# One-hot rows of four tokens: one compare on VectorE and one multiply on GpSimd

## The chip, the core and the metric

The kernel runs on one core of a Trainium2 chip. The metric is the time on the device in microseconds, from the first to the last instruction of one execution and what little lies around them. Three runs of the kernel before took 3524.62, 3525.51 and 3529.61 us; the median is 3525.51.

## What is computed

The reference is a model of two blocks for 512 tokens of width 1024, all in float32. The first block mixes (pooling and a gated delta rule) and then runs a product-key expert layer; the second block is a state-space and attention hybrid. The change lies in the expert layer alone. There every token has 8 heads x 16 = 128 picks; each pick has a first key, a second key (both 0 to 127) and a gate:

```python
experts = jnp.take_along_axis(cand_idx, pos, axis=-1)   # = first * 128 + second
gates = jax.nn.softmax(top_score, axis=-1)
u = jnp.take(expert_down, ei, axis=0)
act = jax.nn.gelu(jnp.einsum("btd,bthkd->bthk", xi, u), approximate=False)
vv = jnp.take(expert_up, ei, axis=0)
return jnp.einsum("bthk,bthkd->btd", gi * act, vv)
```

The kernel does not gather. It computes all 128 x 128 experts for every token and weights them by a gate matrix of 128 x 128 numbers for each token, which is zero but at the token's picks. That matrix is a product of two one-hot matrices. With the 128 picks of a token on the partitions, row p of the one is 1 at pick p's second key, row p of the other is the gate at pick p's first key, and TensorE's product of the two, summed over the picks, is the gate matrix.

## The kernel before

The program is a list of stages. `run` calls each and puts a barrier of all engines behind it, so no instruction of a stage starts before the last one of the stage ahead of it is done. Three stages matter.

`peer_pick` finds the picks of each 128 tokens and transposes them by TensorE, so that picks lie on partitions and tokens along the free dimension: `first`, `second` and `gate`, each 128 x 512. It fills them by three copies out of PSUM (L1443). GpSimd writes `count`, the numbers 0 to 127 in every partition (L1356). In the same stage VectorE compares and multiplies tiles of 128x2048 (L1420, L1427) and reduces them (L1433), while GpSimd subtracts tiles of the weight stream in `split_low` (L162), 128x1024 each.

`peer_gates` is the stage that the change is in. It goes through the 512 tokens four at a time (`QUAD`), 128 steps in all; the buffers `hot1`, `hot2` and four PSUM banks hold four steps. In each step:

- VectorE waits until the product of four steps back is made, then writes the four rows of `hot1`, each by one instruction with two operations, compare `count` with the token's first keys and multiply by its gates (L1498). Keys and gates are scalars of the partition, read from `first` and `gate`. Then it writes the third row of `hot2` by a compare with `second` (L1502).
- GpSimd writes the first two rows of `hot2` by compares (L1487), with scalars from `now`, a copy of the next 16 columns of `second` that it makes itself every fourth step (L1479).
- ScalarE writes the fourth row of `hot2` in two instructions, the absolute distance of the key from the count (L1526) and then 1 minus that, cut at zero (L1532).
- TensorE waits for all three makers and for a free bank, and multiplies, 128x128x128 in float32 for each token (L1517). The profile has two records for each product, so 1024 in all.
- ScalarE copies the bank of four tokens into `stage`, transposed within the partition (L1550). After 32 tokens SyncE stores the 2 MB of `stage` to memory (L1560), from where the next stages load them.

Order within an engine is that of the program: `steps` is a hardware loop whose body has four steps. Everything else is held by semaphores: `product` counts TensorE's steps, `second_made`, `first_made` and `third_made` the makers', `read` the evictions. `past` waits and then counts up a second semaphore of its own engine.

`peer_early` and `peer_experts` follow. They use the stored gate matrices, not `first`, `second` or `gate`.

Of the kernel before, what the change touches and what calls it, by code (L numbers as in the profile page):

```python
# [15 lines left out]
ALU = mybir.AluOpType  # L16
ACT = mybir.ActivationFunctionType
# [5 lines left out]
P = 128  # L23
D = 1024
S = 512
# [1283 lines left out]
QUAD = 4  # L1309
AHEAD = 4 * QUAD  # L1310


def peer_pick(g):
# [7 lines left out]
    g.first = g.at("first", R + 17, [P, S])  # L1321
    g.gate = g.at("gate", R + 18, [P, S])

    g.second = g.at("second", R + 19, [P, S + AHEAD])
# [21 lines left out]
    with ExitStack() as stack:  # L1346
# [5 lines left out]
        with nc.Block() as block:  # L1352
            @block.gpsimd
            def _(pool):
                pool.memset(g.second[:, S:], 0.0)
# [40 lines left out]
            def _(dve):  # L1396
                dve.wait_ge(counted, 1)
                dve.sem_inc(kept, 1)
                with steps(dve, 0, TT, 1) as t:
# [42 lines left out]
                    for r, out in enumerate((g.first, g.second, g.gate)):  # L1442
                        dve.tensor_copy(out[:, bass.ds(t * P, P)], bank[:, r * P:r * P + P]).then_inc(kept, 1)  # L1443
# [6 lines left out]
def peer_gates(g):  # L1450
# [5 lines left out]
    BY_POOL = 2  # L1456
    n_groups = S // GROUP
    g.gates = nc.dram_tensor("gates", [n_groups, P, N_KEYS, GROUP], F32, kind="Internal").ap()
    hot2 = g.at("hot2", R + 21, [P, 4, QUAD, N_KEYS])
    hot1 = g.at("hot1", R + 25, [P, 4, QUAD, N_KEYS])  # L1460
    now = g.at("now", R + 16.5, [P, 4 * QUAD])
    now_read, passed = g.sem("now_read"), g.sem("passed")
    stage = [g.at(f"stage{s}", R + 8 * s, [P, N_KEYS, GROUP]) for s in range(2)]
    second_made, first_made, third_made, product, read, apart, act_passed = (g.sem(x) for x in (
        "second_hot", "first_hot", "second_hot_by_act", "product", "read", "apart", "act_passed"))
    stored = [g.sem(f"stored{s}") for s in range(2)]
    quads = GROUP // QUAD
    with ExitStack() as stack:
        banks = g.banks(stack, 4, "gates")

        with nc.Block() as block:
            @block.gpsimd
            def _(pool):
                pool.sem_inc(product, 4)
                pool.sem_inc(second_made, 1)
                with steps(pool, 0, S // QUAD, 4) as i:

                    pool.wait_ge(second_made, i + 1)
                    pool.tensor_copy(now[:, :], g.second[:, bass.ds(i * QUAD, 4 * QUAD)]).then_inc(now_read, 1)  # L1479
                    pool.wait_ge(now_read, i // 4 + 1)  # L1480
                    for j in range(4):

                        pool.wait_ge(product, i + (j + 1))
                        pool.sem_inc(passed, 1)
                        for k in range(BY_POOL):
                            n = j * QUAD + k
                            ins = pool.tensor_scalar(hot2[:, j, k, :], g.count[:, :], now[:, n:n + 1], None,  # L1487
                                                     ALU.is_equal)
                        ins.then_inc(second_made, 1)

            @block.vector
            def _(dve):
                with steps(dve, 0, S // QUAD, 4) as i:
                    for j in range(4):
                        dve.wait_ge(product, i + (j + 1))
                        for k in range(QUAD):
                            t = i * QUAD + (j * QUAD + k)
                            ins = dve.tensor_scalar(hot1[:, j, k, :], g.count[:, :], g.first[:, bass.ds(t, 1)],  # L1498
                                                    g.gate[:, bass.ds(t, 1)], ALU.is_equal, ALU.mult)
                        for k in range(BY_POOL, QUAD - 1):  # L1500
                            t = i * QUAD + (j * QUAD + k)
                            ins = dve.tensor_scalar(hot2[:, j, k, :], g.count[:, :], g.second[:, bass.ds(t, 1)],  # L1502
                                                    None, ALU.is_equal)

                        ins.then_inc(first_made, 1)
# [16 lines left out]
            def _(act):  # L1522
# [14 lines left out]
                for j in range(4):  # L1537
                    distance(0, j)
                    last_row(0, j)
# [1024 lines left out]
```

## Time and profile before

| | |
|---|---|
| median of three runs | 3525.51 us |
| the profiled execution: its span, first to last instruction | 3527.5 us |
| PE, PEld busy | 3129.7, 2511.6 us |
| DVE, ACT, POOL busy | 1958.1, 1223.1, 446.7 us |
| the gates stage | 1136.8 to 1322.6 us of the span |

The profiled execution has no other time of its own than its span; the span lies between the shortest and the longest of the three runs. PE is TensorE's matmuls, PEld its weight loads, DVE is VectorE, ACT ScalarE, POOL GpSimd and SP SyncE. A busy time is the time in which at least one instruction of the engine was listed as running, waits within the instruction included. In a group of lines the sum after the bar is the busy time, the next number the mean of one instruction in ns, and behind the second bar is the idle time of the engine just before them, with what ended it. A row of the timeline may hold several instructions (x4); its duration is then from the start of the first to the end of the last.

### The profile page before, as it was taken

The page shows a single profiled execution, that of the slowest core. Times are in us where ns is not written, and L with a number is a line of the kernel's source. Part 1 is how long each engine was busy: PE and PEld are TensorE (multiplying, and loading weights), DVE is VectorE, ACT ScalarE, POOL GpSimd, SP SyncE. Part 2 cuts the span into 40 slices and gives each one's busy share as a digit, 9 for nine tenths or more (in the row PEclk, how much of TensorE's full clock was granted, in tenths as well). Part 3 has the DMA queues.
Part 4 walks back from the last instruction along what each step waited for, and adds up shares of the span by engine and source line. Part 5 has one row for each costly group of instructions (what it writes and reads, how often), then busy time and mean ns, then how long its engine had stood idle before and what let it go on. Part 6 is the DMA issues. An engine that isn't in the chain of part 4 may idle for free. (4 is left out here: it accounts for less than half of the span.)

```text
span 3527.5 us, 46718 instructions
## 1 busy us (share of the span) xinstructions
PE 3129.7 (89%) x14568; PEld 2511.6 (71%) x14568; DVE 1958.1 (56%) x3602; ACT 1223.1 (35%) x1758; POOL 446.7 (13%) x656
## 2 busy tenths in 40 slices
PE   6987886996888777999999999999979787888996
PEld 5866784875676666788888888888857566655785
DVE  2555554335999986755555555555554673222232
ACT  3342122432233772222223222222233332466342
POOL 1002333000045990000000000000000130012000
PEclk9999997998998998999999999999989898988998
DMA  2210001321121444433333333333322102200321
GB/s 106 95 65 1 0 0 51 107 94 55 65 84 60 182 175 155 128 122 119 119 119 119 119 119 124 121 122 122 123 84 95 48 25 72 71 0 0 107 95 66
DMA packets 136387, 311.73 MB, mean 88 GB/s; under 512 B 9104, under 2 KB 74768, under 8 KB 134160
## 3 DMA queue, kind: packets, MB, share of 16 engines
q1 hardware_dynamic: 136160, 311.00, 26.0%
q8 instruction: 24, 0.39, 0.0%
q10 hardware_dynamic: 176, 0.11, 0.0%
q14 instruction: 27, 0.22, 0.0%
HBM read 273.33 MB, written 37.75 MB: 88 GB/s over the span
## 5 line engine op out<-in xcount | busy, mean ns | idle before, releaser
L153 ACT ACTIVATE split<-raw 128x1024 fp32r<-128x1024 f32 x440 | 455.7, 1055 | 1250.4 <-PE up L1138 457.6
L162 DVE TENSOR_TENSOR split<-raw,split 128x1024 fp32r<-128x1024 f32 x408 | 491.7, 1224 | 604.6 <-ACT split L153 595.1
L1136 PE MATMUL up<-split,weight_high 128*128 128x512 f32 x1024 | 400.4, 391 | 21.1 <-DVE weight_low L1668 21.1
L1137 PE MATMUL up<-split,weight_high 128*128 128x512 f32 x1024 | 399.1, 390 | 0.0
L1138 PE MATMUL up<-split,weight_low 128*128 128x512 f32 x1024 | 398.9, 390 | 0.0
L1814 DVE TENSOR_TENSOR h<-h,up 128x512 f32<-128x512 f32 x416 | 269.4, 684 | 108.0 <-PE up L1138 108.0
L1750 PE MATMUL down<-xh,split 128*128 128x512 f32 x832 | 323.8, 389 | 1.9 <-ACTq L1771 1.9
L1752 PE MATMUL down<-xh,split 128*128 128x512 f32 x832 | 323.7, 389 | 0.0
L1751 PE MATMUL down<-xl,split 128*128 128x512 f32 x832 | 323.6, 389 | 0.0
L177 PE MATMUL proj<-xh,split 128*128 128x512 f32 x640 | 250.6, 392 | 28.5 <-ACTq L440 28.5
L178 PE MATMUL proj<-xl,split 128*128 128x512 f32 x640 | 250.2, 391 | 0.0
L179 PE MATMUL proj<-xh,split 128*128 128x512 f32 x640 | 250.2, 391 | 0.0
L1136 PEld LDWEIGHTS up<-split,weight_high 128*128 128x128 f32 x1024 | 192.6, 188 | 65.1 <-issue 21.3
L1138 PEld LDWEIGHTS up<-split,weight_low 128*128 128x128 f32 x1024 | 192.5, 188 | 40.2
L1137 PEld LDWEIGHTS up<-split,weight_high 128*128 128x128 f32 x1024 | 192.6, 188 | 39.7
L2048 POOL TENSOR_TENSOR dec<-dec,upto 128x512 f32<-128x512 f32 x16 | 20.1, 1277 | 1490.5 <-ACT dec L2039 1490.5
L1799 DVE TENSOR_TENSOR weight<-gelu,gate 128x512 f32<-128x512 f32 x104 | 72.0, 692 | 246.2 <-ACT gelu L1780 246.2
L1517 PE MATMUL gates<-hot,hot 128*128 128x128 f32 x1024 | 145.6, 290 | 41.0 <-DVE hot L1502 20.6
L1750 PEld LDWEIGHTS down<-xh,split 128*128 128x128 f32 x832 | 156.2, 188 | 34.7 <-ACTq L1771 2.3
L1752 PEld LDWEIGHTS down<-xh,split 128*128 128x128 f32 x832 | 156.2, 188 | 32.4
L1751 PEld LDWEIGHTS down<-xl,split 128*128 128x128 f32 x832 | 156.2, 188 | 32.4
L1517 PEld LDWEIGHTS gates<-hot,hot 128*128 128x128 f32 x1024 | 126.1, 194 | 60.6 <-DVE hot L1502 39.5
(397 smaller groups left out, 5678.0 us busy)
## 6 DMA issues: line engine op xcount, KB each, us to landing
raw<-in_stream SPq DMA_DIRECT2D x440, 512.0 KB, 3.3
gates<-stage SPq DMA_DIRECT2D x16, 2048.0 KB, 6.4
gate<-gates SPq DMA_DIRECT2D x32, 1024.0 KB, 7.5
h<-in_x SPq DMA_DIRECT2D x2, 2048.0 KB, 8.5
rows<-h SPq DMA_DIRECT2D x1, 2048.0 KB, 6.6
h<-rows SPq DMA_DIRECT2D x1, 2048.0 KB, 7.8
out<-res SPq DMA_DIRECT2D x4, 512.0 KB, 2.8
keys<-in_keys SPq DMA_DIRECT2D x1, 1024.0 KB, 4.9
```

Of the source, the lines that this page charges most:

```text
L153: act.activation(g.high[t % slots], g.raw[:, t % RAW, :], ACT.Copy).then_inc(g.high_split, 1)
L162: dve.tensor_tensor(g.low[t % slots], g.raw[:, t % RAW, :], g.high[t % slots], ALU.subtract).then_inc(g.low_split, 1)
L177: pe.matmul(out, hi[:, w], xh[:, c, :], start=(c == 0), stop=False)
L178: pe.matmul(out, hi[:, w], xl[:, c, :], start=False, stop=False)
L1136: pe.matmul(bank, xh, hi[:, w], start=start, stop=False, skip_group_check=True)
L1137: pe.matmul(bank, xh, lo[:, w], start=False, stop=False, skip_group_check=True)
L1138: return pe.matmul(bank, xl, hi[:, w], start=False, stop=stop, skip_group_check=True)
L1517: ins = pe.matmul(banks[j][:, k * P:k * P + P], hot2[:, j, k, :], hot1[:, j, k, :], start=True, stop=True)
L1750: pe.matmul(down[j % 2][:, :], hi[:, k], g.xh[:, c, :], start=(c == 0), stop=False)
L1751: pe.matmul(down[j % 2][:, :], hi[:, k], g.xl[:, c, :], start=False, stop=False)
L1752: last = pe.matmul(down[j % 2][:, :], lo[:, k], g.xh[:, c, :], start=False, stop=(c == DC - 1))
L1814: dve.tensor_tensor(rows, rows, up[n % UP][:, :], ALU.add).then_inc(added, 1)
```

## The change

`first`, `second` and `gate` become one tile `picks` of 128 x 3 x 512, and `hot1` and `hot2` one tile `hot` of 128 x 4 x 2 x 4 x 128 at the same place. In each step VectorE now makes all eight rows of `hot` by one compare of 128x1024, with `count` and the columns of `picks` both spread over the shape by steps of zero. GpSimd waits for that and multiplies the four rows of the first keys in place by the gates, in one instruction of 128x512. TensorE waits for GpSimd's alone. ScalarE writes no rows; it evicts only. `now` and its copy are gone, and so is the memset of the columns behind `second`.

```diff
--- before.py
+++ after.py
@@ -1307,7 +1307,6 @@
 
 
 QUAD = 4
-AHEAD = 4 * QUAD
 
 
 def peer_pick(g):
@@ -1318,10 +1317,8 @@
     nc, base = g.nc, g.base
     g.early = g.at("early", R + 29, [P, EARLY, S])
     hk = HEADS * TOPK
-    g.first = g.at("first", R + 17, [P, S])
-    g.gate = g.at("gate", R + 18, [P, S])
-
-    g.second = g.at("second", R + 19, [P, S + AHEAD])
+
+    g.picks = g.at("picks", R + 17, [P, 3, S])
     g.count = g.at("count", R + 20.25, [P, N_KEYS])
     cand = g.at("cand", R + 21, [P, HEADS, TOPK, TOPK])
     work = g.at("work", R + 25, [P, HEADS, TOPK, TOPK])
@@ -1352,7 +1349,6 @@
         with nc.Block() as block:
             @block.gpsimd
             def _(pool):
-                pool.memset(g.second[:, S:], 0.0)
                 pool.iota(g.count[:, :], pattern=[[1, N_KEYS]], base=0, channel_multiplier=0,
                           allow_small_or_imprecise_dtypes=True).then_inc(counted, 1)
                 with steps(pool, 0, EARLY, 2 * PER) as i:
@@ -1439,8 +1435,8 @@
                                       total[:, 1, :].unsqueeze(2).to_broadcast([P, HEADS, TOPK]),
                                       ALU.mult).then_inc(step, 1)
                     dve.wait_ge(turned, t + 1)
-                    for r, out in enumerate((g.first, g.second, g.gate)):
-                        dve.tensor_copy(out[:, bass.ds(t * P, P)], bank[:, r * P:r * P + P]).then_inc(kept, 1)
+                    for r in range(3):
+                        dve.tensor_copy(g.picks[:, r, bass.ds(t * P, P)], bank[:, r * P:r * P + P]).then_inc(kept, 1)
     g.base += EARLY
 
 
@@ -1453,90 +1449,60 @@
     nc = g.nc
 
 
-    BY_POOL = 2
     n_groups = S // GROUP
     g.gates = nc.dram_tensor("gates", [n_groups, P, N_KEYS, GROUP], F32, kind="Internal").ap()
-    hot2 = g.at("hot2", R + 21, [P, 4, QUAD, N_KEYS])
-    hot1 = g.at("hot1", R + 25, [P, 4, QUAD, N_KEYS])
-    now = g.at("now", R + 16.5, [P, 4 * QUAD])
-    now_read, passed = g.sem("now_read"), g.sem("passed")
+
+    hot = g.at("hot", R + 21, [P, 4, 2, QUAD, N_KEYS])
+    compared, gated, product, read, passed, act_passed = (g.sem(x) for x in (
+        "compared", "gated", "product", "read", "passed", "act_passed"))
     stage = [g.at(f"stage{s}", R + 8 * s, [P, N_KEYS, GROUP]) for s in range(2)]
-    second_made, first_made, third_made, product, read, apart, act_passed = (g.sem(x) for x in (
-        "second_hot", "first_hot", "second_hot_by_act", "product", "read", "apart", "act_passed"))
     stored = [g.sem(f"stored{s}") for s in range(2)]
     quads = GROUP // QUAD
     with ExitStack() as stack:
         banks = g.banks(stack, 4, "gates")
 
         with nc.Block() as block:
+            @block.vector
+            def _(dve):
+                dve.sem_inc(product, 4)
+                with steps(dve, 0, S // QUAD, 4) as i:
+                    for j in range(4):
+
+                        dve.wait_ge(product, i + (j + 1))
+                        at = i * QUAD + j * QUAD
+                        dve.tensor_tensor(hot[:, j, :, :, :], g.count[:, :].unsqueeze(1).unsqueeze(1)
+                                          .to_broadcast([P, 2, QUAD, N_KEYS]),
+                                          g.picks[:, 0:2, bass.ds(at, QUAD)].unsqueeze(3)
+                                          .to_broadcast([P, 2, QUAD, N_KEYS]), ALU.is_equal).then_inc(compared, 1)
+
             @block.gpsimd
             def _(pool):
-                pool.sem_inc(product, 4)
-                pool.sem_inc(second_made, 1)
                 with steps(pool, 0, S // QUAD, 4) as i:
-
-                    pool.wait_ge(second_made, i + 1)
-                    pool.tensor_copy(now[:, :], g.second[:, bass.ds(i * QUAD, 4 * QUAD)]).then_inc(now_read, 1)
-                    pool.wait_ge(now_read, i // 4 + 1)
                     for j in range(4):
-
-                        pool.wait_ge(product, i + (j + 1))
-                        pool.sem_inc(passed, 1)
-                        for k in range(BY_POOL):
-                            n = j * QUAD + k
-                            ins = pool.tensor_scalar(hot2[:, j, k, :], g.count[:, :], now[:, n:n + 1], None,
-                                                     ALU.is_equal)
-                        ins.then_inc(second_made, 1)
-
-            @block.vector
-            def _(dve):
-                with steps(dve, 0, S // QUAD, 4) as i:
-                    for j in range(4):
-                        dve.wait_ge(product, i + (j + 1))
-                        for k in range(QUAD):
-                            t = i * QUAD + (j * QUAD + k)
-                            ins = dve.tensor_scalar(hot1[:, j, k, :], g.count[:, :], g.first[:, bass.ds(t, 1)],
-                                                    g.gate[:, bass.ds(t, 1)], ALU.is_equal, ALU.mult)
-                        for k in range(BY_POOL, QUAD - 1):
-                            t = i * QUAD + (j * QUAD + k)
-                            ins = dve.tensor_scalar(hot2[:, j, k, :], g.count[:, :], g.second[:, bass.ds(t, 1)],
-                                                    None, ALU.is_equal)
-
-                        ins.then_inc(first_made, 1)
+                        past(pool, compared, i + (j + 1), passed)
+                        at = i * QUAD + j * QUAD
+                        pool.tensor_tensor(hot[:, j, 0, :, :], hot[:, j, 0, :, :],
+                                           g.picks[:, 2, bass.ds(at, QUAD)].unsqueeze(2)
+                                           .to_broadcast([P, QUAD, N_KEYS]), ALU.mult).then_inc(gated, 1)
 
             @block.tensor
             def _(pe):
                 with steps(pe, 0, S // QUAD, 4) as i:
                     for j in range(4):
-                        pe.wait_ge(second_made, i + (j + 2))
-                        pe.wait_ge(first_made, i + (j + 1))
-                        pe.wait_ge(third_made, i + (j + 1))
+
+                        pe.wait_ge(gated, i + (j + 1))
 
                         pe.wait_ge(read, i + (j + 1))
                         for k in range(QUAD):
-                            ins = pe.matmul(banks[j][:, k * P:k * P + P], hot2[:, j, k, :], hot1[:, j, k, :],
+                            ins = pe.matmul(banks[j][:, k * P:k * P + P], hot[:, j, 1, k, :], hot[:, j, 0, k, :],
                                             start=True, stop=True)
                         ins.then_inc(product, 1)
 
             @block.scalar
             def _(act):
-                def distance(n, j):
-
-                    t = n * QUAD + (j * QUAD + QUAD - 1)
-                    act.activation(hot2[:, j % 4, QUAD - 1, :], g.count[:, :], ACT.Abs, scale=-1.0,
-                                   bias=g.second[:, bass.ds(t, 1)]).then_inc(apart, 1)
-
-                def last_row(n, j):
-                    act.wait_ge(apart, n + (j + 1))
-                    hot = hot2[:, j % 4, QUAD - 1, :]
-                    act.activation(hot, hot, ACT.Relu, scale=-1.0, bias=1.0).then_inc(third_made, 1)
-
                 act.sem_inc(read, 4)
                 for s in range(2):
                     act.sem_inc(stored[s], 16)
-                for j in range(4):
-                    distance(0, j)
-                    last_row(0, j)
                 with steps(act, 0, n_groups, 2) as i:
                     for s in range(2):
 
@@ -1546,11 +1512,9 @@
                             for j in range(4):
 
                                 past(act, product, n + (s * quads + j + 5), act_passed)
-                                distance(n, s * quads + j + 4)
                                 act.activation(
                                     stage[s][:, :, bass.ds(q * QUAD + j * QUAD, QUAD)],
                                     banks[j][:, :].rearrange("p (t e) -> p e t", e=N_KEYS), ACT.Copy).then_inc(read, 1)
-                                last_row(n, s * quads + j + 4)
 
             @block.sync
             def _(sp):
```

## Rows read from the trace of the kernel before

**Rows 1.** Windows: us, busy us of each engine (x instructions), granted clock, DMA.

```profile
1136.80:1322.60 185.80, 145.61 (x1024) 126.14 (x1024) 173.02 (x640) 139.38 (x392) 170.70 (x288) 0.98 0.40 169
1139.00:1145.00 6.00, 6.00 (x31) 6.00 (x32) 6.00 (x25) 2.90 (x10) 5.58 (x10) 0.55 0.00 1
```

**Rows 2.** Lines of the gates stage: xcount | busy us, mean ns | idle before.

```profile
L1487 POOL TENSOR_SCALAR hot<-count,now 128x128 f32<-128x128 f32 x256 | 162.9, 653 | 7.3 <-POOL now L1479 7.3
L1498 DVE TENSOR_SCALAR hot<-count,first,gate 128x128 f32<-128x128 f32 x512 | 155.3, 367 | 9.2 <-PE gates L1517 8.1 <-PEq L115 1.1
L1550 ACT ACTIVATE stage<-gates 128x512 f32 x128 | 74.0, 578 | 0.0
L1479 POOL COPY now<-second 128x16 f32 x32 | 7.8, 243 | 8.4 <-POOL hot L1487 5.3 <-POOLq L1475 3.1
```

**Rows 3.** Waits of the gates stage: us in total, times, longest.

```profile
PEld gates L1517 <- DVE hot L1502: 39.5, 29, 4.4
PEld gates L1517 <- POOL hot L1487: 15.8, 61, 0.4
PE gates L1517 <- ACT stage L1550: 6.7, 6, 1.1
```

**Rows 4.** Timeline of the gates stage: start us, us, engine, line, what.

```profile
1136.86 1.21 DVE L1498 TENSOR_SCALAR hot<-count,first,gate 128x128 f32<-128x128 f32 x4 [1.10 <-PEq L115]
1143.21 0.58 ACT L1550 ACTIVATE stage<-gates 128x512 f32 x1
1144.91 0.58 ACT L1550 ACTIVATE stage<-gates 128x512 f32 x1
1200.11 1.16 PE L1517 MATMUL gates<-hot,hot 128*128 128x128 f32 x8
1202.01 1.16 DVE L1498 TENSOR_SCALAR hot<-count,first,gate 128x128 f32<-128x128 f32 x4
1322.00 0.58 ACT L1550 ACTIVATE stage<-gates 128x512 f32 x1
```

**Rows 5.** DVE, one line each: xcount: duration min/median/max ns, first and last start.

```profile
L1420 DVE TENSOR_TENSOR hot<-partf,count x8: 2284/2293/4487, 990.0 to 1116.7; 128x2048 f32<-128x2048 f32 x8
L162 DVE TENSOR_TENSOR split<-raw,split x408: 1206/1226/1228, 11.5 to 3494.3; 128x1024 fp32r<-128x1024 f32 x136
```

**Rows 6.** POOL, one line each, same columns.

```profile
L2048 POOL TENSOR_TENSOR dec<-dec,upto x16: 1264/1271/1302, 2791.5 to 2879.7; 128x512 f32<-128x512 f32 x16
L162 POOL TENSOR_TENSOR split<-raw,split x32: 2342/2401/4420, 980.8 to 2886.7; 128x1024 fp32r<-128x1024 f32 x32
L935 POOL COPY win_a<-act x4: 611/611/611, 547.7 to 566.7; 128x512 f32<-128x512 f32 x4
L940 POOL TENSOR_SCALAR pooled<-win_b x2: 1502/1656/1809, 549.5 to 563.2; 128x512 f32<-128x512 f32 x2
```

**Rows 7.** Timeline of the stage before, VectorE and GpSimd.

```profile
997.04 2.29 DVE L1427 TENSOR_TENSOR hot<-hot,keyno 128x2048 f32<-128x2048 f32 x1
997.16 4.42 POOL L162 TENSOR_TENSOR split<-raw,split 128x1024 fp32r<-128x1024 f32 x1 [2.59 <-ACT split L153]
999.25 4.48 DVE L1427 TENSOR_TENSOR hot<-hot,keyno 128x2048 f32<-128x2048 f32 x1
1035.97 2.28 DVE L1420 TENSOR_TENSOR hot<-partf,count 128x2048 f32<-128x2048 f32 x1
1036.29 4.22 POOL L162 TENSOR_TENSOR split<-raw,split 128x1024 fp32r<-128x1024 f32 x1 [2.97 <-ACT split L153]
1038.17 2.48 DVE L1423 TENSOR_TENSOR res<-best 128x128 f32<-128x128 f32 x1
```

**Rows 8.** Timeline of the stage before, one-input reductions beside GpSimd.

```profile
1004.86 4.47 DVE L1433 TENSOR_REDUCE res<-hot 128x128 f32<-128x2048 f32 x2
1008.62 2.34 POOL L162 TENSOR_TENSOR split<-raw,split 128x1024 fp32r<-128x1024 f32 x1 [2.65 <-ACT split L153]
```

**Rows 9.** VectorE's compares of the gates stage, one line, min/median/max ns.

```profile
L1498 DVE TENSOR_SCALAR hot<-count,first,gate x512: 330/341/474, 1136.9 to 1317.4; 128x128 f32<-128x128 f32 x171
```

More of the change, by code:

```diff
@@ L1471, in peer_gates @@
         with nc.Block() as block:
-            @block.gpsimd
-            def _(pool):
-                pool.sem_inc(product, 4)
-                pool.sem_inc(second_made, 1)
-                with steps(pool, 0, S // QUAD, 4) as i:
-                    pool.wait_ge(second_made, i + 1)
-                    pool.tensor_copy(now[:, :], g.second[:, bass.ds(i * QUAD, 4 * QUAD)]).then_inc(now_read, 1)
-                    pool.wait_ge(now_read, i // 4 + 1)
-                    for j in range(4):
-                        pool.wait_ge(product, i + (j + 1))
-                        pool.sem_inc(passed, 1)
-                        for k in range(BY_POOL):
-                            n = j * QUAD + k
-                            ins = pool.tensor_scalar(hot2[:, j, k, :], g.count[:, :], now[:, n:n + 1], None,
-                                                     ALU.is_equal)
-                        ins.then_inc(second_made, 1)
             @block.vector
             def _(dve):
+                dve.sem_inc(product, 4)
                 with steps(dve, 0, S // QUAD, 4) as i:
@@ L1495, in _ @@
                         dve.wait_ge(product, i + (j + 1))
-                        for k in range(QUAD):
-                            t = i * QUAD + (j * QUAD + k)
-                            ins = dve.tensor_scalar(hot1[:, j, k, :], g.count[:, :], g.first[:, bass.ds(t, 1)],
-                                                    g.gate[:, bass.ds(t, 1)], ALU.is_equal, ALU.mult)
-                        for k in range(BY_POOL, QUAD - 1):
-                            t = i * QUAD + (j * QUAD + k)
-                            ins = dve.tensor_scalar(hot2[:, j, k, :], g.count[:, :], g.second[:, bass.ds(t, 1)],
-                                                    None, ALU.is_equal)
-                        ins.then_inc(first_made, 1)
+                        at = i * QUAD + j * QUAD
[3 more added lines that the diff above has]
+                                          .to_broadcast([P, 2, QUAD, N_KEYS]), ALU.is_equal).then_inc(compared, 1)
+            @block.gpsimd
+            def _(pool):
+                with steps(pool, 0, S // QUAD, 4) as i:
+                    for j in range(4):
[4 more added lines that the diff above has]
+                                           .to_broadcast([P, QUAD, N_KEYS]), ALU.mult).then_inc(gated, 1)
             @block.tensor
```

## Prediction

> **What bounds the kernel now.** The page gives PE as the fullest engine of the whole (89%), but that is an average over some twenty stages, and the change touches one, the gates stage. A barrier of all engines stands on either side of it, so what it gains or loses goes one to one into the time. So I looked at that stage alone. It runs from 1136.8 to 1322.6 us of the span, and the windows view says how full each engine is there: of 185.8 us DVE is busy 173.0, POOL 170.7, PE 145.6 and ACT 139.4, at a granted clock of 0.98 [rows 1]. DMA has 0.40 of its engines: no bound.
>
> The stage makes 512 token products, 4 to a step, in 128 steps: 185.8 / 128 = 1.45 us a step. Who sets it? Busy time by step is 173.0 / 128 = 1.35 us for DVE, 1.14 for PE and 1.09 for ACT. POOL's, from the lines view, is its compares with its copy of the next 16 indices and the idle time before either, (162.9 + 7.3 + 7.8 + 8.4) / 128 = 1.46 us [rows 2]: POOL is the full one, DVE 0.1 us behind it. The waits agree: TensorE's weight load waits 39.5 us for DVE's `hot` and 15.8 for POOL's, TensorE 6.7 us for ScalarE's eviction [rows 3]. With both producers below 1.14 us a step PE would be next and the stage could lose at most 1.45 - 1.14 = 0.31 us a step, 40 us in all. That is all the change could win.
>
> **What the two new instructions cost alone.** Removed from each step: on DVE four compares with multiply (L1498, 367 ns each by the lines view, four of them within 1.16 us by the timeline) and one compare, on POOL two compares of 653 ns (and the copy once in four), on ACT two 128-wide activations [rows 2, 4]. ACT is left with the 578 ns eviction; it was not the bound, so this wins nothing by itself. Its prologue of four such pairs, and the memset ahead of the iota in the stage before, go too: under 0.1 us on the path, I take nothing. The three copies that fill `picks` are the three that filled `first`, `second` and `gate`: same shape and number, nothing.
>
> Added on DVE: one TENSOR_TENSOR of 128x1024 fp32 with both inputs broadcast. Rows of the same kind: L1420 is also an is_equal of a broadcast index against the broadcast count, 128x2048, median 2293 ns; L162 on DVE is 128x1024 with two full inputs, median 1226 ns [rows 5]. The slope between them is 1067 / 1024 = 1.04 ns per column, and a broadcast operand shows no extra. So 1.22 us alone.
>
> Added on POOL: one TENSOR_TENSOR mult of 128x512, in place, second operand broadcast. L2048 is a mult in place with a broadcast mask, 128x512: median 1271 ns [rows 6]. Its broadcast is of a middle dimension, the new one of the innermost; no POOL row has that. Bounds from both sides: if the repeated operand were free the row is the one-input copy of 128x512, 611 ns; if it cost as the slowest 128x512 row of POOL, 1656 ns [rows 6]. I take 1.27 us, because operation, type, width and in-place form are those of L2048.
>
> So alone and side by side the step would be 1.27 us, POOL the bound. But they do not run side by side.
>
> **The two new instructions exclude each other.** This is the step that decides. In the stage before this one VectorE and GpSimd both run two-input instructions on SBUF, and the timeline shows what becomes of it [rows 7]. DVE L1427 starts at 997.04 and ends at 999.33 (2.29 us, its usual time). POOL L162 starts at 997.16 and takes 4.42 us instead of its median 2.40 [rows 6]: it ends at 1001.58, 2.25 us after DVE's end. DVE's second L1427 starts at 999.25 and takes 4.48 instead of 2.29: it ends at 1003.73, 2.15 us after POOL's end. Each waited for the whole of the other; nothing was shared. The same stands at 1036 to 1041: DVE L1420 ends at 1038.25, POOL's (4.22 us from 1036.29) at 1040.51, and a DVE instruction of only 128 columns takes 2.48 us, ending at 1040.65, 0.14 us behind POOL. Of a one-input DVE instruction it is not so: two L1433 reductions of 128x2048 take 4.47 us for the pair from 1004.86, 2.24 each, no more than L1420 takes alone, while POOL's L162 from 1008.62 begins beside them and takes its usual 2.34 [rows 8]. And in the gates stage as it is now, DVE's compares with pointer scalars lie between 330 and 474 ns while POOL is busy nearly all the time with compares of 653 ns: no full wait [rows 2, 9]. The kernel of before has in this stage a DVE form that does not exclude POOL; the change puts in its place one that does, for 1024 columns, against a POOL instruction that also has two inputs.
>
> The price of a pair follows from the first case [rows 7]. From DVE's end to DVE's next end, one DVE 2048 and one POOL 1024 took 1003.73 - 999.33 = 4.40 us: 2.25 POOL and 2.15 DVE, both without most of their fixed part, since each has been issued while the other ran. Take off DVE 1024 columns at 1.04 ns: 2.15 - 1.07 = 1.08 us. Take off POOL 512 columns at (2401 - 1271) / 512 = 2.21 ns [rows 6]: 2.25 - 1.13 = 1.12 us. A step is 1.08 + 1.12 = 2.20 us. The upper end is both at their full durations, 1.22 + 1.27 = 2.49, or, with POOL at its slow bound and 0.15 us of either fixed part hidden, 1.08 + 1.51 = 2.59. The lower end, with POOL at the copy's 0.61 less 0.15, is 1.08 + 0.46 = 1.54. I take 2.20: a measured cycle of the same two engines, only scaled in columns.
>
> The Trainium skill, "SBUF — State Buffer", section "SBUF: two separate sides", says that GpSimd and a DVE instruction with two SBUF inputs arbitrate for one pair of ports, which is an exclusive lock held for the whole instruction. On the exclusion the trace agrees (4.42 and 4.48 us above). Read literally, with the fixed parts held as well, it would make a step 2.49 us and the time that of rival 1, below; the 2.15 and 2.25 us after the other's end, against 2.29 and 2.40 alone, speak for about 0.15 us less on either side.
>
> **Does the order of the loop cost more?** The new chain of a step is DVE, POOL, PE, with four buffers. POOL's wait on `compared` and DVE's wait on `product` are queued with nothing else behind them. After the first two steps POOL is always one step behind: while DVE compares n+1, POOL's instruction for n is issued and waits, then while that runs DVE's n+2 waits. DVE's n needs PE's n-4. POOL ended that two cycles earlier, 4.4 us, and PE needs 1.16 us for it [rows 4]. So the order adds no bubble. ACT evicts within 0.6 us. PE is busy 1.14 of 2.20 us, idle about 1 us in each step. That may cost it the clock, 1.2 GHz instead of 2.4. But near the start of the stage, where 0.55 was granted (nearly all of it the lower level), eviction followed eviction after 1.70 us (1143.21 to 1144.91), with all the old producers at work [rows 1, 4]: below 2.20. So the clock does not bind either, and PE's slower products are hidden up to the last.
>
> **The sum.** New stage: 128 x 2.20 = 281.6, plus the first instruction's fixed 0.15, plus the last step's products and eviction, 1.16 + 0.58 and two handoffs of 0.1: 283.7 us. It starts at 1136.86 and so ends at 1420.6; now its last eviction, which the last store needs, ends at 1322.00 + 0.58 = 1322.58 [rows 4]. Difference +98 us. Against the profiled execution's own 3527.5 us that is 3625.5; the median of the runs, 3525.5, lies 2.0 below it (0.06%), which would make 3623.5. I give 3625.
>
> **The rivals.**
> (1) Lock, but with the fixed parts not hidden, or POOL's operand slower: 2.35 to 2.60 us a step, centre 2.49: 128 x 2.49 = 318.7, +135 us, 3661. For: the exact handoff at short instructions is not in the trace, and every one is paid twice in 128 steps. Against: the 0.14 us of the 128-column instruction behind POOL.
> (2) Lock, but POOL cheap with the repeated operand: 1.54 to 2.10 a step, 3540 to 3610. For: the 611 ns copy. Against: L2048, the two-input row of the same width, takes twice that [rows 6].
> (3) Faster: the two do not exclude each other, because both DVE inputs are tiny broadcast sources or POOL's in-place form is of another kind. Then POOL sets the step: 1.27 to 1.30 us, 128 x 1.29 = 165 us against 185.8, -20 us: 3506. It decides once at least 1.27 + 1.22 - 1.45 = 1.04 us of the two durations can lie side by side, so that the step falls below 1.45. For it: the compares of now overlap with POOL's [rows 9]. Against it: L1420, with the same two broadcasts, was the one that POOL waited for at 1036.29 [rows 7].
>
> **How the numbers follow.** Forecast (2.10 to 2.35 a step, 3612 to 3645) 0.65; rival 1 (3645 to 3677) 0.20; rival 2 0.08; rival 3 0.05; the rest 0.02. To leave out no more than 2 in 10 the range takes in the forecast's case and most of rival 1, and at the lower side the slack of POOL's slope: 3600 to 3668. A measurement of this kernel can tell about 0.2%, 7 us, from no change. Faster by over that only in rival 3: 0.05. Within: 0.01. Slower: 0.94.
>
> **What would show it.** In the profile after, the gates stage should last about 284 us, 2.2 us a step. DVE's new line should show about 2.2 us a piece (1.08 of its own and 1.12 of waiting), POOL's about 2.2 us too, both engines nearly 100% busy in the windows view, their busy time mostly waiting. TensorE should wait for POOL's `hot`. All other stages should keep their length. Wrong would be durations of 1.22 and 1.27 with a step of 1.3 (rival 3), durations near 2.5 with a step of 2.5 (rival 1), or gaps between DVE's instructions with PE's `product` as releaser (the order adds a bubble after all).

## The result and the profile after

The changed kernel takes 3600.82 us (median of four runs, 3598.93 to 3605.37), the kernel before in the same comparison 3526.93: a ratio of 1.0212, 95% interval 1.02 to 1.0224. It is slower by 74 us. The forecast was slower, 3625 us, range 3600 to 3668: the measured time lies inside, 0.8 us above the lower end. One execution of a later kernel, the one with both instructions on VectorE in another order, ran at a granted clock of 0.61 and took 5518.04 us; its numbers below are of the other three, at 0.94.

The profiled execution of the changed kernel took 3605.37 us for a span of 3603.3. Its page begins (span; busy us, share of the span and instructions of each engine):

```profile
span 3603.3 us, 45076 instructions
...
PE 3166.6 (88%) x14568; PEld 2540.8 (71%) x14568; DVE 2035.6 (56%) x3090; ACT 1159.6 (32%) x1494; POOL 527.8 (15%) x495
```

The gates stage now runs from the first compare at 1138.27 to the end of the last eviction at 1393.92. The windows view over it (us; busy us of PE, PEld, DVE, ACT, POOL; granted clock, DMA share, GB/s), which answers to the first row of [rows 1]:

```profile
1138.27:1393.92 255.65, 178.20 (x1024) 151.89 (x1024) 251.73 (x128) 76.45 (x128) 252.12 (x128) 0.85 0.29 123
```

255.65 us against 185.7: +69.9 us of the +75.8 us between the two spans. DVE and POOL are both busy for the whole stage, though alone their instructions would need 128 x 1.22 = 156 and 128 x 1.04 = 133 us of it. The remaining 5.9 us lie in front (the stage starts 1.4 us later) and behind: from its end to the end of the span it is 2204.9 us before and 2209.4 here. In the nine kernels of the experiments, where the same stages follow, this stretch takes 2199.8 to 2207.8 us, so most of the difference is scatter. The lines view of the stage, for [rows 2]:

```profile
L1484 POOL TENSOR_TENSOR hot<-hot,picks 128x512 f32<-128x512 f32 x128 | 252.1, 2007 | 7.2 <-DVE hot L1473 7.2
L1473 DVE TENSOR_TENSOR hot<-count,picks 128x1024 f32<-128x1024 f32 x128 | 251.7, 2043 | 1.1 <-DVEq L1467 1.1
L1497 PE MATMUL gates<-hot 128*128 128x128 f32 x1024 | 178.2, 329 | 78.6 <-POOL hot L1484 77.5
L1515 ACT ACTIVATE stage<-gates 128x512 f32 x128 | 76.5, 597 | 185.4 <-PE gates L1497 185.4
```

The waits of the stage, for [rows 3]: TensorE, which waited little, now waits for GpSimd's `hot` in every step.

```profile
PEld gates L1497 <- POOL hot L1484: 105.1, 127, 5.7
PE gates L1497 <- POOL hot L1484: 77.5, 96, 5.3
ACT stage L1515 <- PE gates L1497: 185.4, 128, 11.8
POOL hot L1484 <- DVE hot L1473: 7.2, 1, 7.2
```

The views of the tiles `hot` and `gates` give each line's shortest, median and longest instruction in ns, and its first and last start. For ScalarE's eviction these are 127 steps apart:

```profile
L1473 DVE TENSOR_TENSOR hot<-count,picks x128: 1218/2056/2061, 1138.3 to 1388.0; 128x1024 f32<-128x1024 f32 x128
L1484 POOL TENSOR_TENSOR hot<-hot,picks x128: 1036/2016/2019, 1139.8 to 1390.9; 128x512 f32<-128x512 f32 x128
L1515 ACT ACTIVATE stage<-gates x128: 597/597/599, 1143.9 to 1393.3; 128x512 f32 x128
```

From the last row, (1393.3 - 1143.9) / 127 = 1.96 us a step; the same row before spans 1141.5 to 1322.0, 1.42 us. By GpSimd's starts, (1390.9 - 1139.8) / 127, it is 1.98, the figure that some expectations below use: the first eviction starts 4.1 us after the first multiply, the last one 2.4 us after the last. The longest and the shortest instruction tell most here. In the timeline the first compare, which ran with GpSimd idle, took 1.23 us and the last multiply, with VectorE idle, 1.04; in between they take 2.06 and 2.02, and overlap on paper:

```profile
1138.27 1.23 DVE L1473 TENSOR_TENSOR hot<-count,picks 128x1024 f32<-128x1024 f32 x1 [1.15 <-DVEq L1467]
1197.95 9.97 DVE L1473 TENSOR_TENSOR hot<-count,picks 128x1024 f32<-128x1024 f32 x5
1198.89 7.95 POOL L1484 TENSOR_TENSOR hot<-hot,picks 128x512 f32<-128x512 f32 x4
1200.96 1.16 PE L1497 MATMUL gates<-hot 128*128 128x128 f32 x8 [0.82 <-POOL hot L1484]
1202.94 3.42 PE L1497 MATMUL gates<-hot 128*128 128x128 f32 x13 [0.82 <-POOL hot L1484]
1390.86 1.04 POOL L1484 TENSOR_TENSOR hot<-hot,picks 128x512 f32<-128x512 f32 x1
```

The ends of single instructions from the middle of the stage show what each adds:

```profile
1201.91 2.06 DVE L1473 TENSOR_TENSOR hot<-count,picks 128x1024 f32<-128x1024 f32 x1
1202.85 2.02 POOL L1484 TENSOR_TENSOR hot<-hot,picks 128x512 f32<-128x512 f32 x1
1203.89 2.06 DVE L1473 TENSOR_TENSOR hot<-count,picks 128x1024 f32<-128x1024 f32 x1
```

VectorE ends at 1203.97, GpSimd at 1204.87, VectorE again at 1205.95: 0.90 us for GpSimd and 1.08 for VectorE, each about 0.14 less than alone.

### The profile page after: what moved, and what is told of

Read it like the earlier page. It is cut to its first block and busy times, and to the rows that moved or that the text cites. A ratio compares the mean times of both kernels' runs of the same rounds, so it can differ in the third digit from the quotient of the medians.

```text
span 3603.3 us, 45076 instructions
## 1 busy us (share of the span) xinstructions
PE 3166.6 (88%) x14568; PEld 2540.8 (71%) x14568; DVE 2035.6 (56%) x3090; ACT 1159.6 (32%) x1494; POOL 527.8 (15%) x495
## 5 line engine op out<-in xcount | busy, mean ns | idle before, releaser
L1484 POOL TENSOR_TENSOR hot<-hot,picks 128x512 f32<-128x512 f32 x128 | 252.1, 2007 | 7.2 <-DVE hot L1473 7.2
L1473 DVE TENSOR_TENSOR hot<-count,picks 128x1024 f32<-128x1024 f32 x128 | 251.7, 2043 | 1.1 <-DVEq L1467 1.1
L1497 PE MATMUL gates<-hot 128*128 128x128 f32 x1024 | 178.2, 329 | 78.6 <-POOL hot L1484 77.5
L1497 PEld LDWEIGHTS gates<-hot 128*128 128x128 f32 x1024 | 151.9, 228 | 105.1 <-POOL hot L1484 105.1
L1714 PEld LDWEIGHTS down<-xh,split 128*128 128x128 f32 x832 | 156.6, 188 | 35.1 <-ACTq L1735 2.7
```

The lines of the kernel that those rows point to most:

```text
L1473: dve.tensor_tensor(hot[:, j, :, :, :], g.count[:, :].unsqueeze(1).unsqueeze(1) .to_broadcast([P, 2, QUAD, N_KEYS]), g.picks[:, 0:2, bass. ...
L1484: pool.tensor_tensor(hot[:, j, 0, :, :], hot[:, j, 0, :, :], g.picks[:, 2, bass.ds(at, QUAD)].unsqueeze(2) .to_broadcast([P, QUAD, N_KEYS] ...
L1497: ins = pe.matmul(banks[j][:, k * P:k * P + P], hot[:, j, 1, k, :], hot[:, j, 0, k, :], start=True, stop=True)
L1714: pe.matmul(down[j % 2][:, :], hi[:, k], g.xh[:, c, :], start=(c == 0), stop=False)
```

## The experiments

In all of them a step is read from ScalarE's eviction, last start less first start, over 127. The theory of the forecast is that VectorE's and GpSimd's instructions exclude each other. Its main rival is that the new chain of VectorE, GpSimd and TensorE over four buffers, or the wide instructions themselves, take 1.96 us.

**Take one input of the compare out of SBUF.** VectorE copies `count` into a PSUM bank once and compares from there.

```diff
+        numbers = g.banks(stack, 1, "numbers")[0][:, 0:N_KEYS]
...
+                dve.tensor_copy(numbers, g.count[:, :]).then_inc(copied, 1)
+                dve.wait_ge(copied, 1)
...
-                        dve.tensor_tensor(hot[:, j, :, :, :], g.count[:, :].unsqueeze(1).unsqueeze(1)
+                        dve.tensor_tensor(hot[:, j, :, :, :], numbers.unsqueeze(1).unsqueeze(1)
```

> The changed kernel, with the numbers 0 to 127 copied once into a PSUM bank, from where VectorE's wide compare reads them: the same instruction over the same columns, but with one of its two inputs no longer in SBUF. Theory (VectorE's and GpSimd's two-input instructions on SBUF exclude each other): the exclusion goes, VectorE's instruction takes about 1.2 us and GpSimd's about 1.04 (as its last one did alone), a step 1.15 to 1.25 us, the stage 150 to 162 us, the time about 3495 us, 30 below the kernel before. Rival (the chain VectorE, GpSimd, TensorE over four buffers, or the wide instructions themselves, set the 1.98 us): the step stays near 1.98 and the time near 3600 us.

Measured: 3490.83 us (before 3526.11, ratio 0.9906, interval 0.9889 to 0.9923). Instructions, buffers, order and waits of the loop are those of the changed kernel; only where 128 of the numbers are read from is another. From the lines view:

```profile
L1477 DVE TENSOR_TENSOR hot<-numbers,picks 128x1024 f32<-128x1024 f32 x128 | 145.1, 1211 | 1.1 <-PE gates L1501 0.7 <-DVEq L1471 0.4
L1488 POOL TENSOR_TENSOR hot<-hot,picks 128x512 f32<-128x512 f32 x128 | 133.3, 1041 | 19.8 <-DVE hot L1477 8.6
```

And the line of the eviction:

```profile
L1519 ACT ACTIVATE stage<-gates x128: 597/597/601, 1138.0 to 1281.6; 128x512 f32 x128
```

A step is (1281.6 - 1138.0) / 127 = 1.13 us. Compare and multiply take 1.21 and 1.04 us, as alone, side by side. The chain of waits is not what costs. This kernel is also faster than both the kernel before and the changed one, by 35 us against the kernel before. In the windows view VectorE is now the full engine of the stage (145.1 of 149.1 us busy), and PE looks just as full:

```profile
1133.10:1282.20 149.10, 145.67 (x1024) 125.42 (x1024) 145.07 (x128) 76.50 (x128) 133.29 (x128) 0.98 0.50 211
```

**Leave GpSimd's multiply out.** GpSimd passes the semaphore on, the gates are left out.

```diff
-                        pool.tensor_tensor(hot[:, j, 0, :, :], hot[:, j, 0, :, :], ... ALU.mult).then_inc(gated, 1)
+                        pool.sem_inc(gated, 1)
```

> The changed kernel without GpSimd's multiply by the gates (left out: the gate matrices are counts of picks); GpSimd only passes the semaphore on. Theory: VectorE's compare falls from 2.05 us to about 1.22 with nothing in it changed, a step is 1.15 to 1.2 us (VectorE or TensorE), the time about 3490 us. Rival (VectorE's compare is slow in itself, or the handoffs of the chain are): VectorE's instruction stays above 1.6 us and the time above 3540.

Measured: 3487.46 us. The compare, unchanged, falls from a median of 2056 to 1217 ns, and the step to 1.13 us:

```profile
L1473 DVE TENSOR_TENSOR hot<-count,picks x128: 1214/1217/1226, 1137.8 to 1282.2; 128x1024 f32<-128x1024 f32 x128
L1513 ACT ACTIVATE stage<-gates x128: 597/597/599, 1141.5 to 1285.0; 128x512 f32 x128
```

So the extra 0.84 us in VectorE's instruction is GpSimd's doing, and the multiply in the kernel above is hidden: both kernels have a step of 1.13 us, and the 3 us between their times can't be told from none with one run of this one.

**Both instructions on VectorE.** The multiply stands behind the compare, with a wait on it; GpSimd has no work.

```diff
...
+                        past(dve, compared, i + (j + 1), passed)
+                        dve.tensor_tensor(hot[:, j, 0, :, :], hot[:, j, 0, :, :], ... ALU.mult).then_inc(gated, 1)
```

> The changed kernel with the multiply by the gates on VectorE, right behind its compare with a wait between them; GpSimd idles. Theory: 1.22 + 0.69 us less the overlap of neighbours, 1.75 to 1.9 us a step, the time 3565 to 3585 us: faster than the changed kernel by 15 to 35 us, although one engine does what two did. Rival (no exclusion): two engines' work on one, 1.22 + 0.69 against a true 1.98 that overlapped, so slower than the changed kernel or, if the wide compare takes 2.05 by itself, 2.7 us a step and 3690 us.

Measured: 3607.76 us, ratio 1.0236 (1.0219 to 1.0253), a step of 2.06 us. The theory's forecast failed: this kernel is not faster than the changed one but, as the rival said, a little slower, by 7 us, with intervals that overlap. The rival's ground isn't borne out all the same, since the compare takes 1.22 us here and not 2.05. The timeline shows what was left out of the expectation:

```profile
1199.56 1.22 DVE L1473 TENSOR_TENSOR hot<-count,picks 128x1024 f32<-128x1024 f32 x1
1201.02 0.69 DVE L1478 TENSOR_TENSOR hot<-hot,picks 128x512 f32<-128x512 f32 x1 [0.24 <-DVE hot L1473]
1201.63 1.22 DVE L1473 TENSOR_TENSOR hot<-count,picks 128x1024 f32<-128x1024 f32 x1
```

From compare to compare 2.07 us. The instructions keep their 1.22 and 0.69 us, but between them stands 0.24 us of waiting for VectorE's own result, where neighbours without a wait overlap by their edges. The next kernel takes just this away: in a body of four steps the multiplies of steps 0, 1 and 2 stand behind the compares of 1, 2 and 3, the last one at the end.

```diff
...
+                        for m in ((), (0,), (1,), (2, 3))[j]:
+                            past(dve, compared, i + (m + 1), passed)
...
+                            dve.tensor_tensor(hot[:, m, 0, :, :], hot[:, m, 0, :, :], ... ALU.mult).then_inc(gated, 1)
```

> As e3_mult_dve (both instructions on VectorE, GpSimd idle), but each multiply stands behind the next step's compare (the last two of four steps stand together), so that VectorE doesn't wait for the instruction just ahead. If the 2.06 us of e3_mult_dve were its two instructions plus 0.24 us of idle time on its own result and the overlap lost with it: 1.13 + 0.61 us a step, 1.75, the time about 3567 us. If one of the two instructions is longer next to the other for another reason: it stays at 2.0 and more, 3600 us.

Measured: 3564.60 us (median of three executions, 3564.38 to 3568.29), ratio 1.0112 (1.0092 to 1.0132).

```profile
L1473 DVE TENSOR_TENSOR hot<-count,picks x128: 1214/1215/1226, 1132.6 to 1352.7; 128x1024 f32<-128x1024 f32 x128
L1480 DVE TENSOR_TENSOR hot<-hot,picks x128: 680/680/685, 1134.9 to 1354.4; 128x512 f32<-128x512 f32 x128
L1511 ACT ACTIVATE stage<-gates x128: 597/597/599, 1137.9 to 1356.8; 128x512 f32 x128
```

A step is (1356.8 - 1137.9) / 127 = 1.72 us. One engine doing both pieces of work, ordered so that it doesn't wait, is about 36 us faster than two engines that exclude each other.

**What GpSimd's share of a step is.** The forecast had 1.12 us for it, from rows with other operands. Three kernels put another instruction of 128x512 in the multiply's place; in all three the gates are left out. First, the numbers 0 to 127 repeated along the middle dimension, the form of L2048 in [rows 6]:

```diff
-                                           g.picks[:, 2, bass.ds(at, QUAD)].unsqueeze(2)
+                                           g.count[:, :].unsqueeze(1)
```

> The changed kernel with GpSimd multiplying by the numbers 0 to 127, repeated along the middle dimension, in place of the gates, repeated along the innermost (the gates are left out, the output is another). It asks why GpSimd's share of a step was 0.90 us and not the forecast 1.12. If an operand repeated along the innermost dimension is cheaper for GpSimd: the step goes from 1.98 to about 2.20 us, the stage from 256 to 284 us, the time to about 3629 us. If the forecast's slope of GpSimd was wrong for any form: it stays at 1.98 and 3601 us.

Measured: 3629.84 us.

```profile
L1473 DVE TENSOR_TENSOR hot<-count,picks x128: 1218/2282/2290, 1135.6 to 1413.7; 128x1024 f32<-128x1024 f32 x128
L1484 POOL TENSOR_TENSOR hot<-hot,count x128: 1267/2243/2252, 1137.0 to 1417.1; 128x512 f32<-128x512 f32 x128
L1515 ACT ACTIVATE stage<-gates x128: 597/597/598, 1141.4 to 1420.3; 128x512 f32 x128
```

Then a full operand, the other half of `hot`, without any repeat:

```diff
-                                           g.picks[:, 2, bass.ds(at, QUAD)].unsqueeze(2)
-                                           .to_broadcast([P, QUAD, N_KEYS]), ALU.mult).then_inc(gated, 1)
+                                           hot[:, j, 1, :, :], ALU.mult).then_inc(gated, 1)
```

> The changed kernel with GpSimd multiplying by the rows of the second keys, a full operand of 128x512 without any repeat, in place of the gates (left out). The multiply took 1.04 us alone with the innermost repeat and 1.27 with the middle one. If the innermost repeat is what is cheap: 1.27 us alone and 2.20 us a step, 3629 us. If the middle repeat is what is dear: 1.04 and 1.98, 3602 us.

Measured: 3626.96 us.

```profile
L1473 DVE TENSOR_TENSOR hot<-count,picks x128: 1218/2282/2287, 1137.5 to 1415.5; 128x1024 f32<-128x1024 f32 x128
L1484 POOL TENSOR_TENSOR hot<-hot x128: 1262/2242/2251, 1138.9 to 1418.9; 128x512 f32<-128x512 f32 x128
L1514 ACT ACTIVATE stage<-gates x128: 597/597/598, 1143.3 to 1421.5; 128x512 f32 x128
```

A full operand costs what the middle repeat costs, so it is the innermost repeat that is cheap. Last, a copy of the rows onto themselves, one input:

```diff
...
+                        pool.tensor_copy(hot[:, j, 0, :, :], hot[:, j, 0, :, :]).then_inc(gated, 1)
```

> The changed kernel with GpSimd's multiply replaced by a copy of the same 128x512 onto itself (one input; the gates are left out). If GpSimd's instruction excludes VectorE's two-input one whenever it reads SBUF, whatever its number of inputs: 1.08 + 0.5 = 1.55 to 1.6 us a step, the time about 3543 us. If only two inputs against two exclude each other: 1.13 us a step, 3487 us.

Measured: 3545.09 us.

```profile
L1473 DVE TENSOR_TENSOR hot<-count,picks x128: 1219/1625/1630, 1136.3 to 1332.0; 128x1024 f32<-128x1024 f32 x128
L1484 POOL COPY hot<-hot x128: 612/1602/1608, 1137.7 to 1334.1; 128x512 f32<-128x512 f32 x128
L1513 ACT ACTIVATE stage<-gates x128: 597/597/601, 1141.4 to 1336.4; 128x512 f32 x128
```

Taken together (the shortest instruction is the last one, which ran alone):

| GpSimd's instruction | alone, us | step, us | step less alone |
|---|---|---|---|
| copy, one input | 0.61 | 1.54 | 0.93 |
| multiply, innermost repeat (the change) | 1.04 | 1.96 | 0.92 |
| multiply, full operand | 1.26 | 2.19 | 0.93 |
| multiply, middle repeat | 1.27 | 2.20 | 0.93 |

The step is always GpSimd's own time plus 0.92 to 0.93 us, whatever GpSimd does, one input included: a sum, with next to no overlap. (By GpSimd's own starts the steps are 1.55, 1.98, 2.20 and 2.21 us and the difference 0.93 to 0.94.) Of the two durations alone only 0.3 us is hidden, about 0.15 for each of the two changes of hands in a step. And a multiply whose operand repeats along the innermost dimension takes GpSimd 1.04 us where a full one takes 1.26.

**What a change of hands costs.** The compare is cut into two of 128x512.

```diff
-                        dve.tensor_tensor(hot[:, j, :, :, :], ... [P, 2, QUAD, N_KEYS] ...
+                        for half in range(2):
+                            ins = dve.tensor_tensor(hot[:, j, half, :, :], ... [P, QUAD, N_KEYS] ...
```

> The changed kernel with VectorE's compare cut into two of 128x512, the rest as it is. It asks what a change of hands costs. If the fixed part of an instruction is hidden while the other engine runs and only a VectorE instruction behind a VectorE instruction shows it: 0.55 + 0.61 + 0.91 = 2.07 us a step, the time about 3612 us. If every instruction holds the other off for its full listed duration: 0.69 + 0.69 + 1.04 = 2.4 us, 3655 us.

Measured: 3609.48 us.

```profile
L1474 DVE TENSOR_TENSOR hot<-count,picks x256: 676/688/1526, 1135.4 to 1395.2; 128x512 f32<-128x512 f32 x128
L1486 POOL TENSOR_TENSOR hot<-hot,picks x128: 1041/1243/1247, 1136.9 to 1397.0; 128x512 f32<-128x512 f32 x128
L1517 ACT ACTIVATE stage<-gates x128: 597/597/599, 1140.5 to 1399.4; 128x512 f32 x128
```

A step is (1399.4 - 1140.5) / 127 = 2.04 us, 0.08 more than with one compare. The timeline shows in which order the pieces run (the last row holds two halves):

```profile
1200.66 1.52 DVE L1474 TENSOR_TENSOR hot<-count,picks 128x512 f32<-128x512 f32 x1
1202.45 1.23 POOL L1486 TENSOR_TENSOR hot<-hot,picks 128x512 f32<-128x512 f32 x1 [0.82 <-DVE hot L1474]
1202.10 2.12 DVE L1474 TENSOR_TENSOR hot<-count,picks 128x512 f32<-128x512 f32 x2
```

A second half ends at 1202.18. The first half of the next compare starts at 1202.10 and, at 0.68 us, ends at about 1202.78, 0.60 later. GpSimd's multiply comes between the two halves and ends at 1203.68, 0.90 later; the second half ends at 1204.22, 0.54 later. The half behind VectorE's own instruction adds 0.06 us more than the half behind GpSimd; GpSimd's 0.90 is as before. The full durations, 2.4 us, are not what an engine holds the other off for.

**Who holds the faster kernels at 1.13 us.** As in the kernel without the multiply, but the compare makes only the rows of the first keys, and TensorE multiplies them by themselves. Second keys and gates are left out.

```diff
-                        dve.tensor_tensor(hot[:, j, :, :, :], ... g.picks[:, 0:2, bass.ds(at, QUAD)] ...
+                        dve.tensor_tensor(hot[:, j, 0, :, :], ... g.picks[:, 0, bass.ds(at, QUAD)] ...
-                            ... hot[:, j, 1, k, :], hot[:, j, 0, k, :],
+                            ... hot[:, j, 0, k, :], hot[:, j, 0, k, :],
```

> As e2_no_mult, with VectorE comparing the rows of the first keys alone, 128x512, and TensorE multiplying them by themselves (the second keys and the gates are left out). It asks who holds e1_count_psum and e2_no_mult at 1.13 us a step. If VectorE (its instruction follows every 1.13 us): the step falls to what TensorE needs, 1.09 us or less, the time by 5 us or more to 3480. If TensorE: nothing changes, 1.13 us and 3486.

Measured: 3461.00 us, a step of (1253.8 - 1138.4) / 127 = 0.91 us. The eviction, the windows view of the stage, and two compares of the timeline, 0.90 us apart, before which VectorE now waits for TensorE:

```profile
L1513 ACT ACTIVATE stage<-gates x128: 597/597/598, 1138.4 to 1253.8; 128x512 f32 x128
1135.20:1254.40 119.20, 117.48 (x1024) 117.29 (x1024) 88.39 (x128) 76.42 (x128) 0.00 (x0) 0.97 0.63 264
```

```profile
1200.14 0.69 DVE L1473 TENSOR_TENSOR hot<-count,picks 128x512 f32<-128x512 f32 x1 [0.20 <-PE gates L1495]
1201.04 0.69 DVE L1473 TENSOR_TENSOR hot<-count,picks 128x512 f32<-128x512 f32 x1 [0.20 <-PE gates L1495]
```

VectorE was the bound at 1.13, by more than expected. TensorE's products take 117.5 us of the stage here; before, at the same number of products, it was listed as busy for 145.6 us. Two things change in this kernel, the compare and the operands of the products, so it can't tell by itself whether TensorE is as fast with two different operands. The weight loads of the kernels with different operands can: first the kernel before, then the one with the numbers in PSUM, last this one.

```profile
1200.11 0.97 PEld L1517 LDWEIGHTS gates<-hot,hot 128*128 128x128 f32 x8 [0.31 <-POOL hot L1487]
1199.94 0.97 PEld L1501 LDWEIGHTS gates<-hot 128*128 128x128 f32 x8 [0.18 <-POOL hot L1488]
1199.84 4.77 PEld L1495 LDWEIGHTS gates<-hot 128*128 128x128 f32 x42
```

One load takes 0.19 us, so they start (0.97 - 0.19) / 7 = 0.11 us apart in the first two and (4.77 - 0.19) / 41 = 0.11 in the third: 8 of them need 0.89 us a step in all three kernels, at granted clocks of 0.97 and 0.98, and in the kernels at 1.13 the loads wait for their producer in between. TensorE's records overlap, and the 8 of a step end 1.16 us after the first begins [rows 4]; that time, not the need, is what the listed busy time adds up.

## Why the prediction was right, and where it missed

- **What bounds the stage now.** GpSimd first, VectorE close behind, was argued from busy times, and no run tested it by itself. What could be won at most was wrong: 0.31 us a step took PE's listed busy time, 1.14 us, for its need. The last experiment has 0.90, and the weight loads are as close together with two different operands, so the room was 0.55 us a step, 70 us.
- **VectorE's instruction alone: 1.22 us.** Right: 1.21 to 1.23 in every kernel where it stood alone. That a broadcast operand adds nothing was right too.
- **GpSimd's instruction alone: 1.27 us.** This term was mis-sized: it measured 1.04. L2048 was the nearest row, but its repeat lies in the middle dimension, the new one in the innermost. The prediction named this as the thing that no row had, and kept 0.61 as the lower end; the truth lay between.
- **The exclusion.** Right, and it decides the sign. The kernel with the numbers in PSUM takes the cause away and changes nothing else in the loop, and 110 us go with it.
- **The price of a pair.** 1.08 + 1.12 = 2.20 us was forecast; the middle of the stage has 1.08 + 0.90 = 1.98. With the operand that the forecast had in mind the step is 2.20 and the time 3629.84, so the scaling of the 4.40 us pair [rows 7] holds to a hundredth, and what was too much is GpSimd's term alone, 1.12 for 0.90: 128 x 0.22 = 28 us, and the stage is 28 us shorter than forecast (255.65 against 283.7). The time was missed by 24 us; in the profiled execution the stages around took 5.9 us more than before, most of it scatter.
- **The range.** The step, 1.96 to 1.98 us, and the time lie outside the forecast's own case (2.10 to 2.35 us, 3612 to 3645, chance 0.65) and inside that of rival 2, which was given 0.08. The range held by 0.8 us, and one of the four executions, 3598.93, lies below it. That the time fell inside is luck in part; the sign and its reason are not.
- **The order of the loop adds no bubble, the clock doesn't bind.** Right: VectorE has no idle time before its compares after the first, and the granted clock did fall to 0.85 in the stage without a mark on the step.
- **Rival 1 (nothing of the fixed parts hidden, or a slower operand)** fell with the step itself, 1.96 to 1.98 where the full durations make 1.22 + 1.04 = 2.26, and with the cut compare: 2.04, not 2.4. The Trainium skill, "SBUF — State Buffer", section "SBUF: two separate sides", says that the lock is held for the whole instruction. As to blocking, each run with both inputs of the compare in SBUF agrees: the copy with one input blocks as well. As to the time, about 0.15 us of an instruction's listed duration does lie beside the other's, at either change of hands.
- **Rival 2 (a cheap repeated operand)** is what happened, near its upper end (1.54 to 2.10 us a step, 3540 to 3610): against the full operand the repeat saves 0.22 us, and the copy, its lower end, would have saved 0.65. Why the innermost repeat is cheaper, no run shows.
- **Rival 3 (no exclusion)** is out. What it described was seen only with the numbers in PSUM, and there the step is 1.13.
- **The profiled execution.** The text set its sum against the span, 3527.5. The runs behind it show that an execution's time is about 2 us more than its span (3605.37 for 3603.3).

## What to carry over

Before work is moved from VectorE to GpSimd "to share it", look at the inputs of the VectorE instruction beside it: with two in SBUF the times of the two engines add up but for 0.3 us a pair, and here the split cost more than it saved. A small constant operand in PSUM, or a form with scalars of the partition, keeps both running; here the operand in PSUM is the difference between 74 us slower and 35 us faster. The sign is seen in advance in any stage of the same trace where both engines run two-input instructions: durations that are the sum of both, ends that follow each other.

## What the runs showed of the hardware beyond that

- GpSimd's multiply of 128x512 in float32 takes 1.04 us when one operand repeats along the innermost dimension and 1.26 us with a full one; a copy takes 0.61 us.
- A pair of 128x1024 on VectorE, both inputs in SBUF, and 128x512 on GpSimd takes the sum of the two durations alone less 0.3 us, with one input on GpSimd too.
- VectorE compares 128x1024 at the same speed with one input in PSUM (1210 ns) as with both in SBUF (1217).
- A wait of VectorE on the instruction just ahead of it costs 0.24 us of idle time and the overlap of neighbours: 2.06 against 1.72 us a step for the same two instructions.
- TensorE's listed busy time in a stage that waits for others overstates its need: 145.6 us listed, 117.5 with products that hardly wait. The starts of its weight loads, 0.11 us apart in both, give the need.
